# A PEER layer on one core: parts of v become the stationary operand, and the coefficients of 192 tokens stream

## The reference

```python
experts = e1 * N_KEYS + e2                    # 8 heads x 16 experts a token, of 128*128
g = jax.nn.softmax(top_s, axis=-1)
act = jax.nn.gelu(jnp.einsum('td,thkd->thk', x_tok, peer_u[experts]), approximate=False)
coef = act * g
f = jnp.einsum('thk,thkd->td', coef, peer_v[experts])
x = layer_norm(DEEPNORM_ALPHA * x + f, ln2_g[l], ln2_b[l])
```

## Time and profile before

| | |
|---|---|
| three runs | 1905.19, 1906.56, 1913.26 us (median 1906.56) |
| profiled execution | 1898.23 us, its span 1896.4 us |
| TensorE busy | 1779.9 us, 94% |
| VectorE busy | 1363.7 us, 72% |
| ScalarE busy | 855.4 us, 45% |
| GpSimd busy | 670.2 us, 35% |
| moved by DMA | 433.27 MB, 228 GB/s in the mean |

### The profile page before, as it was taken

The page is one execution under the profiler, slowest core; times in us unless marked ns, Lnnn a source line. Parts: engine busy times, 40 slices in busy tenths (PEclk is TensorE's granted clock), DMA queues, the critical chain, the costliest instruction groups (busy, mean ns, idle before and its releaser), DMA issues.

```text
span 1896.4 us, 33625 instructions
## 1 busy us (share of the span) xinstructions
PE 1779.9 (94%) x12090; PEld 1627.9 (86%) x12090; DVE 1363.7 (72%) x1903; ACT 855.4 (45%) x1212; POOL 670.2 (35%) x425
## 2 busy tenths in 40 slices
PE   8999999899999999999999999969695999999996
PEld 8999978899999999999999999847574777777875
DVE  7998985699937777777764445557483787888866
ACT  5544444444444444444444444524242445444443
POOL 0000024678961000000000000677786787777201
PEclk9999999999999999999999999989897999999999
DMA  7665556555566555555556565769695999999863
GB/s 277 225 211 191 184 167 215 189 173 175 170 209 229 183 182 186 183 181 188 181 189 194 191 193 191 230 201 332 220 346 187 383 350 369 332 348 366 293 210 114
DMA packets 137934, 433.27 MB, mean 228 GB/s; under 512 B 34304, under 2 KB 34432, under 8 KB 136320
## 3 DMA queue, kind: packets, MB, share of 16 engines
q1 hardware_dynamic: 97440, 359.97, 55.9%
q0 software_dynamic: 22528, 67.16, 9.7%
q10 hardware_dynamic: 17888, 5.26, 1.2%
HBM read 423.83 MB, written 8.39 MB: 228 GB/s over the span
## 4 chain that ended last, share of the span: by engine, by line
PE 71%; POOL 11%; issue 8%; DMA 5%; DVE 4%; ACT 2%; SPq 0%; DVEq 0%; POOLq 0%; ACTq 0%
PE psum L1409 18%; PE psum L1410 18%; PE psum L1411 18%; POOL rows L532 5%; DMA raw<-in_v_w_dram 4%; POOL sp_act L538 4%; PE psum L1576 3%; PE psum L1578 2%; PE psum L1577 2%; PE psum L1580 2%; PE psum L1581 2%; DVE w_lo L815 2%; PE psum L1543 1%; PE psum L1453 1%; PE psum L1455 1%
## 5 line engine op out<-in xcount | busy, mean ns | idle before, releaser
L575 ACT ACTIVATE w_hi<-raw 128x1024 fp32r<-128x1024 f32 x652 | 691.2, 1061 | 936.4 <-PE psum L1411 484.3
L815 DVE TENSOR_TENSOR w_lo<-raw,w_hi 128x1024 fp32r<-128x1024 f32 x568 | 688.6, 1224 | 310.3 <-ACT w_hi L575 303.3
L1409 PE MATMUL psum<-xt_hi,w_hi 128*128 128x256 f32 x2944 | 827.1, 281 | 15.5 <-DVE xt_lo L829 9.3
L1410 PE MATMUL psum<-xt_lo,w_hi 128*128 128x256 f32 x2944 | 824.6, 280 | 0.0
L1411 PE MATMUL psum<-xt_hi,w_lo 128*128 128x256 f32 x2944 | 823.7, 280 | 0.0
L1409 PEld LDWEIGHTS psum<-xt_hi,w_hi 128*128 128x128 f32 x2944 | 555.2, 189 | 17.4 <-issue 11.5
L1411 PEld LDWEIGHTS psum<-xt_hi,w_lo 128*128 128x128 f32 x2944 | 555.1, 189 | 0.0
L1410 PEld LDWEIGHTS psum<-xt_lo,w_hi 128*128 128x128 f32 x2944 | 555.0, 189 | 0.0
L532 POOL DMA_INDIRECT rows<-in_v_w_dram,sp_idx x256 | 364.4, 1423 | 148.1 <-issue 101.6
L538 POOL DMA_INDIRECT sp_act<-act_spill,sp_idx x64 | 78.6, 1228 | 626.2 <-DMA act_spill<-stage 585.5
L1576 PE MATMUL psum<-w_hi,c_hi 128*128 128x512 f32 x504 | 204.3, 405 | 78.9 <-DVE w_lo L815 76.7
(11 more groups left out here) (193 smaller groups left out, 1165.1 us busy)
## 6 DMA issues: line engine op xcount, KB each, us to landing
raw<-in_u_w_dram SPq DMA_DIRECT2D x256, 512.0 KB
raw<-in_v_w_dram SPq DMA_DIRECT2D x256, 512.0 KB
raw<-in_w_in_dram SPq DMA_DIRECT2D x80, 512.0 KB
raw<-in_w_out_dram SPq DMA_DIRECT2D x32, 512.0 KB
raw<-in_w_q_dram SPq DMA_DIRECT2D x32, 512.0 KB
act_spill<-stage ACTq DMA_DIRECT2D x32, 128.0 KB, 2.3
rows<-in_v_w_dram,sp_idx POOLq DMA_INDIRECT x256
xt_raw<-in_x_t_dram SPq DMA_DIRECT2D x4, 512.0 KB, 7.5
```

The costliest lines, as they stand in the source:

```text
L575: nc.scalar.activation(parts_of(slot_u)[0][:, :], raw[:, slot_u % RAW, :], ACT.Copy).then_inc(hi_done, 1)
L815: tt(lo_w[:, :], raw[:, slot_u % RAW, :], hi_w[:, :].bitcast(f32), ALU.subtract).then_inc(lo_done[slot_u % SPLIT], SPLIT)
L1409: mm(dst, hi_w[:, sl], xt_hi[:, kk, :], start=st, stop=False)
L1410: mm(dst, hi_w[:, sl], xt_lo[:, kk, :], start=False, stop=False)
```

## The change

In the down projection the operands trade places. A tile of 128 features of v is now the stationary operand and the 192 tokens' coefficients are the moving one; a key tile needs four feature tiles q with three matmuls each. The result has the features on the partitions, and two feature tiles share a PSUM bank. `c_both` and the fold are gone; a coefficient set has two parts of 192 columns. Each chunk's sums are copied to `y_t` by ACT (feature tiles 0 and 1) and DVE (2 and 3), and TensorE transposes them back, eight 128x128 transposes a chunk. The sparse tokens' sums are no longer folded in: one half of `picked` is added to the residual in place, the other is brought to the right partitions by a DMA and then added. In the last chunk the feature tiles 0 and 1 come first and 2 and 3 after them, and both token blocks are normalized after the last matmul. POOL's activations after the first 16 are issued one or two behind each pick, and the picks stand at other units.

```diff
-    return U_DOWN + 14 + (U_LAST - U_DOWN - 16) * k // PICKS
+    return U_DOWN + 20 + (U_LAST - U_DOWN - 18) * k // PICKS
+def acts_issued(k):
+    return min(PICKS, PICKS_IN + (4 * max(0, k - ROWS + 1) + 2) // 3)
...
-            return [sb(f"{name}_{part}", [P, GROUP, P], f32r, where) for part in ("hi", "lo", "both")]
+            return [sb(f"{name}_{part}", [P, GROUP, TD], f32r, where) for part in ("hi", "lo")]
...
+        def v_tile(j, q):
+            return v_bank(j, q // 2)[:, q % 2 * T:q % 2 * T + TD]
...
-            for n in range(1, PICKS // PICKS_IN):
-                gather_acts(n)
-                for k in range(ROWS + 8 * (n - 1), ROWS + 8 * n):
-                    gather_rows(k)
-            for k in range(ROWS + 8 * (PICKS // PICKS_IN - 1), PICKS):
+            for k in range(ROWS, PICKS):
                 gather_rows(k)
+                gather_acts(acts_issued(k - 1), acts_issued(k))
+            pool.wait_ge(picked_done, PICKS)
+            nc.gpsimd.dma_start(rows[2][P - SPARSE:P, :], picked[0:SPARSE, :]).then_inc(half_in, 16)
+            for i in range(2):
+                nc.gpsimd.memset(y_t[i][:, :, TD:T], 0.0).then_inc(y_zero, 1)
...
-                nc.scalar.activation(hi_c[:, :, :], hid[:, mine, 0:P], ACT.Copy).then_inc(chi_done, 1)
-                nc.scalar.activation(both_c[:, :, 0:TD - P], hid[:, mine, P:TD], ACT.Copy).then_inc(chi_done, 1)
+                nc.scalar.activation(hi_c[:, :, :], hid[:, mine, :], ACT.Copy).then_inc(chi_done, 1)
...
-                nc.scalar.activation(y_part[j % 2][0][:, :], v_bank(j, 1), ACT.Copy).then_inc(split_hi, 1)
-                nc.scalar.activation(s_part[j % 2][0][:, :], picked[:, j * DCH:(j + 1) * DCH], ACT.Copy)\
-                    .then_inc(split_hi, 1)
+                nc.scalar.activation(y_t[j % 2][:, 0:2, 0:TD], v_tiles(j, 0), ACT.Copy).then_inc(y_first, 1)
...
-            def split_low(j):
-                dve.wait_ge(split_hi, 2 * j + 2)
...
+            def second_sums(j):
+                if j >= 2:
+                    dve.wait_ge(y_tr, TB * (j - 1))
+                if j == 0:
+                    dve.wait_ge(picked_done, PICKS)
+                dve.wait_ge(used, USED0 + U_LAST + 2 * LAST * (j + 1))
+                nc.vector.tensor_copy(y_t[j % 2][:, 2:4, 0:TD], v_tiles(j, 1)).then_inc(y_second, 1)
+            def add_picked(n):
...
+                stt(res[mine, TB - 1, :], part[mine, :], 1.0 / ALPHA, res[mine, TB - 1, :],
+                    ALU.mult, ALU.add).then_inc(res_added, 1)
...
-                    if 0 in blocks:
-                        mm(v_bank(j, 0), hi_c[:, n, :], w1, start=st, stop=False)
-                        mm(v_bank(j, 0), hi_c[:, n, :], w2, start=False, stop=False)
-                        i = mm(v_bank(j, 0), lo_c[:, n, :], w1, start=False, stop=en)
-                    if 1 in blocks:
-                        mm(v_bank(j, 1), both_c[:, n, :], w1, start=st, stop=False)
-                        i = mm(v_bank(j, 1), both_c[:, n, :], w2, start=False, stop=en)
+                    for q in tiles:
+                        sl = slice(e * DCH + q * P, e * DCH + (q + 1) * P)
+                        st = first and h == 0 and e == 0 and q % 2 == 0
+                        en = last and h == 1 and e == 1 and q % 2 == 1
+                        mm(v_tile(j, q), hi_w[:, sl], hi_c[:, n, :], start=st, stop=False)
+                        mm(v_tile(j, q), hi_w[:, sl], lo_c[:, n, :], start=False, stop=False)
+                        i = mm(v_tile(j, q), lo_w[:, sl], hi_c[:, n, :], start=False, stop=en)
...
-            def fold_chunk(j):
-                pe.wait_ge(split_lo, 2 * j + 2)
...
+            def transpose_chunk(j):
+                pe.wait_ge(y_zero, 2)
+                pe.wait_ge(y_first, j + 1)
+                pe.wait_ge(y_second, j + 1)
+                for b in range(TB):
+                    transpose_sums(j, b, range(4)).then_inc(y_tr, 1)
...
+            pe.wait_ge(y_second, j + 1)
+            transpose_sums(j, 0, range(2, 4)).then_inc(y_tr, 1)
+            transpose_sums(j, 1, range(4)).then_inc(y_tr, 1)
```

More of the change, by code:

```diff
@@ L243, in build @@
         hid = sb("hid", [P, N_KEYS, TD], f32)
[L247 to L250, removed]
+        sums = ExitStack()
+        y_t = [sb(f"y_t{i}", [P, DCH // P, T], f32, sums) for i in range(2)]
+        sums.close()
         rows = [sb(f"rows{i}", [P, D], f32) for i in range(2)] + rows_late
@@ L290, in v_bank, with v_tiles @@
             return bank[(2 + 2 * j + b) % 8]
+        def v_tile(j, q):
+            return v_bank(j, q // 2)[:, q % 2 * T:q % 2 * T + TD]
+        def v_tiles(j, half):
+            return v_bank(j, half).rearrange("p (q t) -> p q t", t=T)[:, :, 0:TD]
         USED0, GLU0, S0, TAPS0 = 1, 2, 2, 1
@@ L389, in build @@
         coef_at = {down_unit(g, 0): g + 1 for g in range(GROUPS - 1)}
-        split_at = {U_LAST + 2 * LAST * (j + 1) + 3: j for j in range(NCH - 2)}
-        split_at[U_LAST + 2 * LAST * (NCH - 1) + 5] = NCH - 2
         PER_HEAD = 2 * 11 + 2 + 12
@@ L534, in gather_rows, with gather_acts @@
                         bass.IndirectOffsetOnAxis(sp_idx[:, 1 + j, k:k + 1], 0)).then_inc(rows_in[k % ROWS], 16)
-            def gather_acts(n):
-                for k in range(PICKS_IN * n, PICKS_IN * (n + 1)):
+            def gather_acts(first, end):
+                for k in range(first, end):
                     nc.gpsimd.indirect_dma_start(
                         sp_act[:, k:k + 1], None, act_dram,
-                        bass.IndirectOffsetOnAxis(sp_idx[:, 0, k:k + 1], 0)).then_inc(act_in[n], 16)
+                        bass.IndirectOffsetOnAxis(sp_idx[:, 0, k:k + 1], 0)).then_inc(act_in[k // PICKS_IN], 16)
             pool.wait_ge(idx_done, 1)
@@ L776, in _ @@
                     coef_hi(coef_at[u])
-                if u in split_at:
-                    split_high(split_at[u])
-            split_high(NCH - 1)
+                if u > U_LAST + 2 * LAST and (u - U_LAST) % (2 * LAST) == 1:
+                    first_sums((u - U_LAST) // (2 * LAST) - 1)
+            first_sums(NCH - 1)
             n_normed = 0
-            for turn, b in enumerate((1, 0)):
+            for turn, b in enumerate((0, 1)):
                 act.wait_ge(ln_var, TB + turn + 1)
@@ L1292, in pick @@
                 i.then_inc(picked_done, 1)
-            def split_low(j):
-                dve.wait_ge(split_hi, 2 * j + 2)
-                tt(y_part[j % 2][1][:, :], v_bank(j, 1), y_part[j % 2][0][:, :].bitcast(f32),
-                   ALU.subtract).then_inc(split_lo, 1)
-                tt(s_part[j % 2][1][:, :], picked[:, j * DCH:(j + 1) * DCH], s_part[j % 2][0][:, :].bitcast(f32),
-                   ALU.subtract).then_inc(split_lo, 1)
+            def second_sums(j):
[6 more added lines that the diff above has]
+            def add_picked(n):
+                mine = slice(P - SPARSE, P)
+                if n == 0:
+                    dve.wait_ge(picked_done, PICKS)
+                    dve.wait_ge(res_in, 16)
+                    part = picked
+                else:
+                    dve.wait_ge(half_in, 16)
+                    dve.wait_ge(res_added, 1)
+                    part = rows[2]
+                stt(res[mine, TB - 1, :], part[mine, :], 1.0 / ALPHA, res[mine, TB - 1, :],
+                    ALU.mult, ALU.add).then_inc(res_added, 1)
             onehot1(0)
@@ L1594, in group @@
                         n = 2 * j + h
-                        down(U_DOWN + 2 * NCH * g + n, U_DOWN + n, j, h, c_sets[slot], [0, 1], first)\
+                        down(U_DOWN + 2 * NCH * g + n, U_DOWN + n, j, h, c_sets[slot], range(4), first)\
                             .then_inc(used, 1)
```

159 lines of the change are left out of this document (71 added, 88 removed).

## The result

The changed kernel takes 2033.14 us (median of four runs, 2019.71 to 2036.36; a fifth on record took 2046.69); the kernel before, run beside it, 1909.32. The ratio is 1.0652 [1.0587, 1.0717]: slower, as forecast, but by 6.5% and not by 1.2%. The profiled execution took 2019.71 us with a span of 2017.9. It was forecast at 1921, so 99 us have to be found.

What follows compares the result with a forecast made beforehand. TensorE's matmuls were taken to bound the kernel, with POOL's issues close by. Matmuls 688.1 + transposes 3.6 + waits 25 = 716.7 against 696.6 us, +20.1, with the end +23: median 1930 us, range 1876 to 1954.

Steps and rivals of the forecast that it cites:

- The matmuls: Down projection on TensorE: 6144 matmuls of 192 columns at 112 ns each, 688.1 us, 90.6 more than before.
- Rival 1: Down-projection matmuls: columns stay the measure, 87.5 ns; POOL becomes the bound, 22 to 48 us faster, median 1859 to 1885; chance 0.20.
- rival 2: Down-projection matmuls: weight load takes all of 116.7 ns, +42 us, 1949; chance 0.72 together with the forecast.
- rival 4: Down-projection matmuls: narrow f32r handled like plain float32, 336 ns for 192 columns, some 1370 us more; chance 0.04.
- Transposes, copies, the end: Down projection and kernel end: transposes 3.6 us replace the folds' 3.7, copies 0, 12.3 us behind the last matmul, plus 3.
- The waits: Down projection: the even spread of gathers leaves 25 us of waits of the 95.4, with ends 5 and 65.
- the outer end: Upper end of the down projection's waits: 65 us, at 2.0 us an issue and with clock losses.
- 192 issues x 1.83 = 351 us: POOL's gathers for picks 4 to 39: 144 rows and 48 activations at 1.83 us each, 351 us, to 1591.
- Rival 3: POOL's gathers: POOL stays behind, 2.0 us an issue beside a DVE that never rests; waits 65, 1970 us; chance 0.04.
- Rival 5: TensorE in the down projection: the granted clock might fall; argued against, no size, given no chance of its own.
- an end of about 17 us: Sign that the prediction is right: the kernel's end is about 17 us long.
- 163 of each 205: DVE's load in the earlier trace: busy 163 us of each 205 at most, with more time per unit after the change.

Runs made afterwards that it cites:

- experiment 8: Changed kernel with dynamic_dma_scratch_size 2048, down-projection matmuls streaming 128 of the 192 columns: 1896.66 us in one execution, 2254.67 in the other.
- 9: Changed kernel with dynamic_dma_scratch_size 2048 and stationary weights of 64 of the 128 features, all 192 columns streamed: 1867.16 us, ratio 0.9784.
- experiment 2: Changed kernel with dynamic_dma_scratch_size 2048 in place of 1024 and `sp_act` moved: 1893.79 us, ratio 0.9929 to the kernel before.
- (5): Changed kernel with dynamic_dma_scratch_size 768 in place of 1024: 2174.46 us, ratio 1.1403 to the kernel before.
- experiment 1: Changed kernel without the 48 activation DMAs behind the first 16, coefficients formed from those 16: 1894.45 us, ratio 0.9931 to the kernel before.
- (3): Changed kernel with POOL's old gather order, 16 activations at a time behind picks 3, 11 and 19: 1920.63 us, ratio 1.0071.
- 4: Kernel before, operands not swapped, with the changed kernel's gather order and pick units: 2013.23 us, ratio 1.0564.
- 7: Kernel before with the even spread of the gathers and dynamic_dma_scratch_size 2048: 1870.03 us, ratio 0.9792.

## Why the prediction was wrong

**The matmuls: right.** I took 112 ns against 87.5 by columns. In the stretch 1760 to 1884 us, dense and at full clock, 1113 matmuls take 124.00 us, 111.4 ns each; 6144 of them make 684.4 us where I had 688.1. The reason was right too: experiments 8 and 9 show that the 128 weight columns set the pace, not the stream (111 ns with 192 streamed columns and with 128, 90 ns with 64 weight columns). The rows that I used were for plain float32, and their 111 to 112 ns are those of f32r as well. Rival 1, rival 2 and rival 4 fall.

**Transposes, copies, the end: right.** The last matmul is over at 2001.58 us and DVE at 2013.53:

```profile
2001.69 0.56 DVE L1298 COPY y_t<-psum 128x384 f32<-128x384 f32 x1 [12.05 <-PE psum L1586]
...
2012.13 1.40 DVE L902 SCALAR_TENSOR_TENSOR res<-psum,rstd,ln2b 128x512 f32<-128x512 f32 x2
```

That is 11.9 us against 9.4 before, plus 2.5 where I had plus 3.

**The waits: wrong, and it is the whole miss.** The stage lasts from 1184.5 to 2001.6, 817.1 us. Less 684.4 and the 3.6 of the transposes, 129.1 us are waits and slow clock; I had 25, with 65 as the outer end. Over the four stretches TensorE is idle for 20.7 + 47.7 + 0 + 1.0 = 69.4 us. The other 59.7 are matmuls at the low clock, where they stand 213 ns apart instead of 111 (seven starts from 1499.74 to 1501.02 us, at a clock of 0.50). The step that failed is "192 issues x 1.83 = 351 us". They took from 1245 to 1692 us, 447 us, 2.33 us each. The 1.83 came from the old order and was used as if the price of an issue were its own. It is not: from the start of the first lump POOL issues only seven indirect DMAs at this setting before it stops, and in the spread order its pace is set by such stops, 25 of them between 1386 and 1712 us. In the old order fifteen row DMAs (1265.48 to 1287.70 us) went out behind a lump without a gap, and of its twelve gaps of 1 us or more up to 1440 us eight, with 23.9 of 31.9 us, stand in front of an activation. The spread put activations, and with them a stop of 4.0 us in the mean, into every period.

That the room is the cause is shown from two sides, by more of it (2) and by less (5). That it is the spread of the activations which runs out of it is shown by leaving them out (1), by the old order (3) and by the new order in the old kernel, without and with more room (4 and 7). That a stop holds back the pick is read in the timeline. The rest of the sum held: without waits it gives 688.1 + 3.6 against 696.6 and 3 at the end, 1896 us for a profiled execution, and experiment 2, whose TensorE has no holes, took 1893.81. Rival 3 named the outcome, "POOL stays behind, each issue costing 2.0 us", but with DVE's company as the reason, with 65 us of waits, 1970 us, and a chance of 0.04. DVE's company is refuted: in experiment 2 POOL has the same company of DVE and of row DMAs (from 1480 to 1760 us DVE is busy for 209.39 us, the DMA engines for 90%) and keeps up: TensorE is busy for all of the 280 us.

**The clock: wrong in its kind.** Rival 5's argument against a falling clock was that the holes of before were up to 23 us long and that no gap here would exceed 25 ns. With holes of 3.0 us in the mean and 5.4 at most, 22 of them up to 1760 us, the granted clock was 0.81 to 0.84 over some 340 us. So a small wait was paid nearly twice (129.1 us for 69.4 of idle time). The 25 us that I took had nothing for that; only the outer end, 65, named the clock.

**Two slips that changed nothing.** The prediction's last paragraph wants an end of about 17 us, where its own sum has 12.3; it took 11.9. And DVE's busiest stretch in the earlier trace rows is 227 of 280 us, 81%, which is a little over the "163 of each 205".

**What hid it.** The earlier trace rows gave 1.83 us an issue, but an issue with its gap to the next is 1.25 us there where nothing disturbs it (0.95 and 0.30). I put the difference down to lumps and DVE. The row that would have told is one that I did not quote: in the trace of before, the first lump stops for 3.43 us behind its seventh DMA, too.

Open: what gives the room back, and why the stops come where activation DMAs, each with a 512-byte result, stand between the rows. It is not the count of packets. POOL's queue over the whole execution, on the page of the changed kernel and on that of experiment 1, which has 48 activations less (packets, MB, share):

```profile
q0 software_dynamic: 22608, 67.69, 9.4%
...
q0 software_dynamic: 21072, 67.66, 9.5%
```

The difference is 1536 packets, 32 for each activation; by the 22528 of the kernel before, less 64 x 32, each of the 256 row DMAs has 80. So an activation is fewer packets than a row DMA, and its issue is as long (0.95 us undisturbed). Yet the kernel stops where activations stand between the rows: some 129 us beyond the usual distances in front of row DMAs, against some 17 in experiment 1 (79.9 us for 211 issues), where POOL also waits for picks. At 20 of the 25 stops that end between 1386 and 1712 us all packets of the DMAs issued so far had gone before POOL went on, as in the first lump; no run here says why.

## What to carry to other kernels

The price of an issue taken from one order need not hold in another with the same count (1.83 us became 2.33 here): look first for gaps that no instruction explains, and count how many DMAs had gone out at the first of them. Try a larger `dynamic_dma_scratch_size` before the order is judged: here 2048 for 1024 turned 6.5% slower into 0.7% faster. A matmul with 128 weight columns of its own went by its stream at 512 and 256 columns (233.5 and 116.7 ns) and stood at 111 ns at 192 and at 128, so a swap of operands that shortens the stream to less than about 245 columns (an estimate, 111.4/0.456) buys nothing for the columns below that. Short waits that came again and again cost clock as well as time here (59.7 us on top of 69.4); add what the low clock costs before calling them small.

## What was not expected of the hardware

- The number of indirect DMAs that POOL issues before it first stops goes with `dynamic_dma_scratch_size`: 5 at 768, 7 at 1024, 14 at 2048, and this was worth 6.9% here (2033.14 to 1893.79 us). If each takes an equal part of the setting, it is 137 to 146 of it (an estimate: 2048/15 and 1024/7).
- The granted clock fell in experiment 8 with TensorE almost never waiting (for `w_lo` twice in the down projection, 1.3 us in all). Two stretches of 20 us in its profile:

```profile
1420.00:1440.00 20.00, 20.00 (x182) 20.00 (x180) 11.89 (x9) 6.03 (x6) 15.87 (x13) 1.00 0.99 373
1440.00:1460.00 20.00, 18.91 (x99) 18.77 (x98) 12.65 (x9) 8.04 (x8) 13.76 (x12) 0.58 0.91 302
```

There is one wait of 1.1 us, which ends at 1443.3; behind it the clock is 0.50 and stays there up to some 2200 us, near the end of the down projection, with TensorE busy all the time. In the other execution it did not happen (mean clock 0.995), nor in any of the eight of experiment 2, with 192 columns (0.994 or 0.995). Why the clock did not come back sooner is open.
- At the low clock the matmuls with their own weights stand some 210 ns apart, for 192 columns (213, the changed kernel at 1500 us) and for 128 (experiment 8 at 1600 us) alike; at the full clock it is 111 for both.
- Of the changed kernel, the issue of POOL that ends each of the 25 stops between 1386 and 1712 us begins beside a pick of DVE and lasts 2.69 to 2.72 us instead of 0.94 (the one at 1506.95 us ends at 1509.65, its pick at 1508.83). The issue at 1716.93 us, which no stop precedes, also begins beside a pick (1716.86) and lasts 0.95. No run shows what makes the 25 longer.
